# Feed-forward stages of a four-layer kernel: up-tile products of 256 columns interleaved with products of 512 columns

## The reference

```python
def conv_ffn(x, w_up, conv_w, w_down):
    h = causal_dwconv(x @ w_up, conv_w)
    g, v = jnp.split(h, 2, axis=-1)
    return (jax.nn.silu(g) * v) @ w_down

def conv_ffn_2(v, w_in, conv_w, conv_b, w_out):
    gate, up = jnp.split(v @ w_in, 2, axis=-1)
    hid = jax.nn.gelu(dwconv_centred(gate, conv_w, conv_b)) * up
    return hid @ w_out
```

## Time and profile before

| | |
|---|---|
| Median of 3 runs | 1359.43 us (1358.23 to 1359.77) |
| Time of the profiled execution | 1358.28 us |
| Span of the profiled execution | 1357.0 us |
| TensorE busy | 1333.3 us, 98% of the span |
| VectorE busy | 1021.8 us, 75% |
| ScalarE busy | 783.4 us, 58% |
| Mean granted TensorE clock | 0.999 of full speed |

### The profile page before, as it was taken

One profiled execution on the slowest core, in us unless ns is written; L12 is line 12 of the kernel. 1 busy time (PEld: TensorE's weight loads), 2 busy tenths in 40 slices (PEclk: granted clock), 3 DMA queues, 4 the chain that ended last, 5 costly groups with the idle time before them and its releaser, 6 DMA issues. The chain is left out here.

```text
span 1357.0 us, 20751 instructions
## 1 busy us (share of the span) xinstructions
PE 1333.3 (98%) x8197; PEld 1159.0 (85%) x8197; DVE 1021.8 (75%) x1683; ACT 783.4 (58%) x1268; POOL 148.0 (11%) x131
## 2 busy tenths in 40 slices
PE   7999999999999999999999999999999999999998
PEld 6887888888898788887987888888789998888887
DVE  5876588777897788778788677776567997786766
ACT  5654266565443565563677566555557875655553
POOL 4770300000100000000000000000302224000000
PEclk9999999999999999999999999999999999999999
DMA  8623255655563556553542255655344344455551
GB/s 312 236 78 125 90 221 216 234 186 186 195 248 124 187 186 240 195 193 117 213 168 100 114 205 203 220 194 197 135 170 173 131 150 187 155 188 205 194 197 71
DMA packets 38575, 242.17 MB, mean 178 GB/s; under 512 B 4432, under 2 KB 7376, under 8 KB 11088
## 3 DMA queue, kind: packets, MB, share of 16 engines
q1 hardware_dynamic: 38480, 240.86, 48.3%
HBM read 236.89 MB, written 2.64 MB: 177 GB/s over the span
## 5 line engine op out<-in xcount | busy, mean ns | idle before, releaser
L319 DVE TENSOR_TENSOR wlo<-raw,whi 128x2048 fp32r<-128x2048 f32 (+1 forms) x179 | 401.1, 2246 | 102.4 <-ACT whi L296 100.3
L296 ACT ACTIVATE whi<-raw 128x2048 fp32r<-128x2048 f32 x195 | 370.4, 1903 | 83.7 <-PE ps L471 40.0
L408 PE MATMUL ps<-XS,whi 128*128 128x512 f32 x1392 | 331.7, 390 | 0.0
L408 PEld LDWEIGHTS ps<-XS,whi 128*128 128x128 f32 x1392 | 257.8, 188 | 52.0 <-issue 0.6
L460 PE MATMUL ps<-whi,MS 128*128 128x512 f32 x960 | 233.5, 391 | 0.0
L460 PEld LDWEIGHTS ps<-whi,MS 128*128 128x128 f32 x960 | 177.5, 188 | 35.8 <-issue 0.4
L413 PEld LDWEIGHTS ps<-XS,wlo 128*128 128x128 f32 x1392 | 178.5, 191 | 6.8
L413 PE MATMUL ps<-XS,wlo 128*128 128x256 f32 x1392 | 180.6, 283 | 0.0
L388 PE MATMUL ps<-XS,whi 128*128 128x256 f32 x672 | 167.5, 289 | 0.0
L389 PE MATMUL ps<-XS,whi 128*128 128x256 f32 x672 | 163.8, 283 | 0.0
L304 POOL TENSOR_TENSOR wlo<-raw,whi 128x512 fp32r<-128x512 f32 x90 | 124.5, 1414 | 191.1 <-ACT whi L296 103.1
(11 more groups left out here) (331 smaller groups left out, 1541.9 us busy)
## 6 DMA issues: line engine op xcount, KB each, us to landing
raw<-in_up SPq DMA_DIRECT2D x88, 1024.0 KB, 4.8
raw<-in_down SPq DMA_DIRECT2D x44, 1024.0 KB, 4.9
raw<-in_hg_t SPq DMA_DIRECT2D x16, 1024.0 KB, 4.8
raw<-in_od_t SPq DMA_DIRECT2D x8, 1024.0 KB, 5.6
raw<-in_ev_a SPq DMA_DIRECT2D x6, 1024.0 KB, 9.5
raw<-in_wa_o SPq DMA_DIRECT2D x6, 1024.0 KB, 5.0
raw<-in_hg_o SPq DMA_DIRECT2D x6, 1024.0 KB, 4.9
raw<-in_ev_o SPq DMA_DIRECT2D x4, 1024.0 KB, 5.9
```

What stands on the lines that cost most here:

```text
L296: ac.activation(parts_of(m)[0][:, 0:w], raw[m % NRAW][:, 0:w], ACT.Copy).then_inc(w_hi)
L319: ve.tensor_tensor(lo[:, c], r[:, c], hi[:, c].bitcast(F32), ALU.subtract).then_inc(w_lo_v)
L408: pe.matmul(banks[i][:, 0:512], hi[:, c], XS[:, k, 0:512], start=(k == 0), stop=False)
```

## The change

The products of one up tile are put in another order, and nothing is added or removed. The 256-column products of the first block (`lo`, banks[0]) stand one by one behind the 512-column products of the second block. The 256-column products of the second block are given back as a function `second_low`. It is called, one k at a time, behind the first eight 512-column products that TensorE does next: those of the next up tile's first block, or the first eight high products of the down tile that follows. `w_done` of an up tile is raised by its last product as before, so it now comes eight pairs into the following tile. `banks[1]` is begun by the 512-column products of the second block, as before.

```diff
-        def project_wide(m, banks, ready=None):
+        def project_wide(m, banks, ready=None, before=None):
             hi = high(m)
-            for i in range(2):
-                for k in range(8):
-                    if ready and i == 0:
-                        ready(k)
-                    c = slice(1024 * i + 128 * k, 1024 * i + 128 * k + 128)
-                    pe.matmul(banks[i][:, 0:512], hi[:, c], XS[:, k, 0:512], start=(k == 0), stop=False)
+            for k in range(8):
+                if ready:
+                    ready(k)
+                pe.matmul(banks[0][:, 0:512], hi[:, 128 * k:128 * k + 128], XS[:, k, 0:512], start=(k == 0), stop=False)
+                if before:
+                    before(k)
             lo = low(m)
-            for i in range(2):
-                for k in range(8):
-                    c = slice(1024 * i + 128 * k, 1024 * i + 128 * k + 128)
-                    last = pe.matmul(banks[i][:, 0:256], lo[:, c], XS[:, k, 0:256], start=False, stop=(k == 7))
-            last.then_inc(w_done)
+            for k in range(8):
+                pe.matmul(banks[1][:, 0:512], hi[:, 1024 + 128 * k:1152 + 128 * k], XS[:, k, 0:512], start=(k == 0), stop=False)
+                pe.matmul(banks[0][:, 0:256], lo[:, 128 * k:128 * k + 128], XS[:, k, 0:256], start=False, stop=(k == 7))
+
+            def second_low(k):
+                ins = pe.matmul(banks[1][:, 0:256], lo[:, 1024 + 128 * k:1152 + 128 * k], XS[:, k, 0:256], start=False, stop=(k == 7))
+                if k == 7:
+                    ins.then_inc(w_done)
+
+            return second_low
...
-            def with_high(some, hs, tt):
+            def with_high(some, hs, tt, before=None):
+                done = 0
...
+                            if before and done < 8:
+                                before(done)
+                            done += 1
...
-                    with_high(every, whole, tt)
+                    with_high(every, whole, tt, None if tt else before)
...
         def ffn_pe(k):
...
-                    project_wide(ffn_up(k, j), up_banks(k, j), xs_both(n) if j == 0 else None)
+                    second_low = project_wide(ffn_up(k, j), up_banks(k, j), xs_both(n) if j == 0 else None, second_low)
                 if m > 1:
                     d = m - 2
                     accumulate([ffn_down(k, d)], MS, [2 * d % 8, (2 * d + 1) % 8], 1024, accs,
-                               lambda c, tt, d=d: ready(2 * d + 1, tt) if c == 2 * d % 8 else None, d == 0, False)
+                               lambda c, tt, d=d: ready(2 * d + 1, tt) if c == 2 * d % 8 else None, d == 0, False, before=second_low)
+                    second_low = None
```

More of the change, by code:

```diff
@@ L431, in project_first, with accumulate @@
             project(0, o, blocks=(1,))
-        def accumulate(tiles, S, ks, n, accs, ready, first, last, halves=False):
+        def accumulate(tiles, S, ks, n, accs, ready, first, last, halves=False, before=None):
             per = 2048 // n
```

## The result

| | before | after |
|---|---|---|
| Median | 1359.6 us (4 runs) | 1375.01 us (4 runs, 1374.33 to 1376.9) |
| Ratio of the two | | 1.0116, 95% interval 1.0104 to 1.0128 |
| Profiled execution, time | 1358.28 us | 1374.33 us |
| Its span | 1357.0 us | 1373.0 us |
| TensorE busy | 1333.3 us | 1344.4 us |

The change costs 15.4 us by the medians (16.0 between the two profiled executions). The forecast was +5.3 us, slower, with a range up to 1373.0 us, so the sign was right and the size was not.

What follows compares the result with a forecast made beforehand. The prediction took TensorE, busy 98% of the span, as the bound. Its terms, -1.6 for pairs, +1.9 for first tiles and +5.0 for last chunks, gave +5.3 us on 1359.43, so 1364.7 us, range 1355.5 to 1373.

Steps and rivals of the forecast that it cites:

- What bounds the kernel: Whole kernel: TensorE, busy 98% of the span, is the bound; the two reordered kinds of product take 38% together.
- The rival of the free pairs: Up tiles: a long-short pair takes 340 ns, products -9.9 us, total 1357.4 us, not slower; chance 0.19.
- the 13.3 ns: Each product: time beyond its columns at 2.4 GHz, taken as the cost of a load beside it, once per load.
- Part 1, the new pairs: Up tiles: 1392 pairs at 346 ns plus 1.0 us of recovery against 484.2 us before, -1.6 us.
- My bound for a long product: Up tiles: a long product behind a short one takes at least 226.7 and at most 236 ns.
- the recovery: Long products after short ones: 0.027 us lost, paid where alternation ends in plain long products, 4 x 9 down tiles, 1.0 us.
- The rival of the unsettled pairs: Up tiles: pairs never settle, 232 + 120 = 352 ns, products +6.8 us, total 1373.1 us; chance 0.20.
- Part 2, the first tiles: Tile 5 of stages 0 and 1: VectorE stays as late, 0.96 us still owed, +1.9 us; nothing in stages 2 and 3.
- Part 3, the last chunk: End of each stage: late `w_done` of tile 21 makes TensorE wait on chunk 21, 2 x 1.4 + 2 x 1.1 = +5.0 us.
- the credit of 0.49 us: Stage 0's end: VectorE's L319 is over before tile 21's addition, so the chain falls from 8.48 to 7.99 us.
- my own sum: Stage 0's end: chain 7.99 + 0.17 - 6.83 us of TensorE's products, a wait of 1.33 us.
- The rival without waits: Both waiting places: VectorE's and ScalarE's queues move up, leaving the products alone, 1357.8 us; chance 0.15.

Runs made afterwards that it cites:

- kicks: alt_in_tile with a few products out of step, another pattern per stage, at each alternation behind a down tile from tile 6 on; 1365.27 us, one run.
- the kick: The changed kernel, alternations behind plain long products beginning long, short, short, short, long, long; 1369.54 us, ratio 1.0073 to the kernel before.
- in_time: The changed kernel, second block's low products not held back in tiles 0-4 of stages 0 and 1 and every tile 21; 1373.44 us, ratio 1.0101.
- late_block: The changed kernel's late `w_done`, but low products in blocks of eight, nothing alternating; 1369.61 us, ratio 1.0072 to the kernel before.
- alt_in_tile: The kernel before with each up tile as 16 long-short pairs, all inside the tile, `w_done` at its end; 1368.83 us, ratio 1.0070.

## Why the prediction was right and wrong, point by point

**What bounds the kernel, and that a load behind a load is not the limit of a short product: right as far as it went.** No alternation gave a pair of 340 ns or less for longer than the first one. The rival of the free pairs had named exactly this hope, and it is shown wrong in every kernel that alternates. The Trainium skill (TensorE: Matmul & The Clock Gate, Part 2, on LDWEIGHTS) says that a load runs ahead through a port of its own. Taken alone, that gives the order of products with identical loads no price. In these runs it has one, since the same products take 346.7 or 353.3 ns a pair; whether the load has a part in that, no run shows. Whether the 13.3 ns really come from the load was only argued, since no run took a load away.

**Part 1, the new pairs: the step that failed.** "I take 113 + 233 = 346, because both are the rows of exactly these neighbours." That gave -1.6 us; measured are +8.1 us. The two rows were first products behind a *settled* run of the other kind. In an alternation no product has a settled run in front of it, and the products keep a memory over several others: kicks shows it. From a settled run of long products the pairs fall into a cycle of three that averages 353.3 ns. The rows of before held a warning: the long products behind a short run took 233, 236, 229, 232 and 231 ns and not one dear product followed by cheap ones. My bound for a long product, 236 ns, did not hold either: every third one takes 241. I read the recovery as a bounded one of 0.027 us and not as the sign of a state that an alternation might never leave. The rival of the unsettled pairs did name that, at 352 ns and 1373.1 us, and was nearly right in size: a mean of 352.1 ns, though in a cycle of 353.3 ns and not as 232 + 120. It had 0.20 of the chance. Most of what it lacks to 8.1 us is the recovery behind an alternation. The eight long products behind one lose some 50 ns in all, 1.8 us over the kernel, where I had put 1.0. With its +6.8 us, or the 8.1 measured, in place of -1.6 the sum would have been 1373.1 or 1374.4 us, against 1375.0.

**Part 2, the first tiles: right in place and nearly in size.** Forecast 1.9 us in stages 0 and 1; measured 0.72 + 0.90, and 0.30 + 0.07 in stages 2 and 3, where I had taken nothing: 2.0 us. In stage 0 the slow pairs had used up some of the time that TensorE would have waited: with the kick the waits there are 0.97 us. In stage 1 the pairs before the first wait took 346.7 ns with and without the kick, and the waits are 0.90 us both times. So that the total is within 0.1 us of the forecast is partly luck.

**Part 3, the last chunk: right, a little small.** Forecast 5.0 us, measured 1.70 + 1.69 + 1.09 + 1.09 = 5.6. The step that was off is the credit of 0.49 us. "With `w_done` later that work is over" was wrong: tile 20's `w_done` is late by the same 2.77 us, so VectorE is still in L319 (335.88 to 338.17) and takes up the addition 1.02 us after tile 21's end at 337.07. The chain was 8.40 us, not 7.99, and with my own sum (8.40 + 0.17 - 6.83) that is a wait of 1.74 us, where 1.70 was measured. in_time shows that same queue at its worst.

**The rival without waits: shown wrong** by the 7.5 us of new waits in the changed kernel, and by late_block, where they cost without any alternation.

## What to carry to other kernels

Price an order of products from rows of that very order. The first product behind a settled run says little about an alternation, so when no row shows the pattern, the unsettled average would have been a better middle here than the best pair of neighbours. An engine that is idle a quarter of the time can have no slack at all at two places of a stage, and a completion signal moved by 2.77 us is paid there. When undoing a late signal, look at the iteration queued in front too: tile 21 in time took nothing off the wait on chunk 21 until tile 20 was in time too.

## What the runs showed of the hardware that was not expected

The pace of fp32r products, each with its own load of 128 columns, has a memory. Settled runs take 226.7 ns (512 columns) and 120 ns (256 columns). Pairs of the two fall into one of three cycles: three pairs in 1060 ns (233 + 117, 241 + 120, 236 + 113), two pairs in 693 ns (233 + 117, 231 + 113), or one in 346.7 ns (230 + 117). Each holds until something disturbs it. In the changed kernel 34 of 36 alternations began behind settled long products, and all 34 fell into the first cycle. The other two are those of tile 0 in stages 1 and 2. A wait stands just before the eight long products ahead of them, and these had not settled (224 to 236 ns up to the last); both alternations ran in the second cycle. Tile 0 of stage 0 also stands behind a wait, but there the long products had settled at 227 ns. Behind a stop the instructions alone don't decide: alt_in_tile and kicks have the same products up to tile 5, and tile 0 of stage 1 went on at 346.7 ns a pair in the one and 353.3 in the other. In the changed kernel a stop of some 0.07 to 0.5 us changed the cycle at least once in each stage, in one direction or the other. The mean granted clock was 0.995 to 1.000 in all these runs. In windows inside the four feed-forward stages it was 1.00, the upper level of 2.4 GHz, in the kernel before, in the changed kernel and in kicks alike, so it is not the clock that makes the difference. What in TensorE or its reads keeps this memory is open. So is whether it hangs on the widths at all: wherever the width changed in these alternations, the stationary operand changed between `whi` and `wlo` too, and no run separates the two.
